# Down weights of the expert layers loaded by GpSimd's queue in place of SyncE's

## The chip, the cores and the metric

The kernel runs on one core of a Trainium2 chip. The metric is the device time of one execution in microseconds (us). A core has five engines that run their own instruction streams and meet at semaphores: TensorE (PE, with PEld for its weight loads), VectorE (DVE), ScalarE (ACT), GpSimd (POOL) and SyncE (SP). SyncE, ScalarE and GpSimd can each issue DMA transfers; every issuer has a queue of its own, and 16 DMA engines move the data of all of them.

## The reference, cut to what matters

One inference step of a two-layer decoder trunk on 512 prompt tokens and 8 sample tokens, 1024 wide, all in float32. Layer 0 mixes tokens by latent attention, layer 1 by causal pooling; each layer then applies a mixture of 16 experts, of which a router picks two per token:

```python
def moe(x, w_router, router_bias, w_gate, w_up, w_down):
    B, S, D = x.shape
    t = x.reshape(B * S, D)
    combine = route(t, w_router, router_bias).astype(x.dtype)
    h = jax.nn.silu(jnp.einsum('td,edf->tef', t, w_gate)) * jnp.einsum('td,edf->tef', t, w_up)
    y = jnp.einsum('tef,efd->td', h * combine[:, :, None], w_down)
    return y.reshape(B, S, D)
```

Per expert and layer, w_gate and w_up are 1024 x 512 and w_down is 512 x 1024, 2 MB each. After each part, x becomes LayerNorm(ALPHA * x + f(x)).

## The kernel before, in words

The kernel writes each engine's stream by hand, one function per engine (`sp`, `pe`, `pool_e`, `act`, `dve`), with semaphores between them. No scheduler changes the order: an engine executes what its function issues, in that order.

The expert part of a layer works in tiles. A tile is 96 token rows (CAP) of one expert. Sixteen tiles are the sixteen experts; further tiles take the rows of experts with more than 96, which these inputs don't need in this trace (16 tiles a layer, 8 turns of a loop over `u` with `s` = 0, 1 in it, tile number 2u + s).

- Routing (VectorE, `route`) makes the row numbers, the table `tile_ids` and the count `n_half`. GpSimd then scatters the token rows to `expert_rows` in HBM by ten indirect transfers (line 1087).
- ScalarE's queue loads the rows of a tile in four pieces (line 1256), VectorE transposes them (1724).
- TensorE does for each tile the gate product (line 919, with eight transposes of the tile before at 905 in its midst), the up product (929) and the down product (940). VectorE and ScalarE form silu(gate) * up, copy results out of PSUM, and ScalarE's queue stores the tile's rows to `expert_out` (1281).
- After a layer's last tile GpSimd gathers two rows per token from `expert_out` (1107 in layer 0, 1116 in layer 1) and the norm follows.

The weights lie in two buffers, `ring[0]` and `ring[1]`, each with room for one gate, one up and one down matrix (`wg`, `wu`, `wd`). Tile (u, s) reads buffer 1 - s. Each third is loaded again as soon as its product is done: `gate_ps`, `up_ps` and `down_ps` count TensorE's finished products, and `wg_ld`, `wu_ld`, `wd_ld` count what has landed, 16 per transfer. TensorE waits for `wd_ld` ahead of the down product. So a transfer is issued two tiles ahead of its use.

All three are issued by SyncE in `load_expert` (line 464): wait until the gate third is free, issue gate (468), wait, issue up (472), wait, issue down (476). The first two experts of a layer are loaded ahead of the loop (483, 484 in layer 0, 493 and 499 in layer 1). The gate and up loads read 16 KB runs of HBM per partition (`"a (p k) f -> p (a k) f"`), the down load four rows of 4 KB (`"a (k p) d -> p (a k) d"`). In layer 1, SyncE waits for the gathers to land (492) before the first expert, and for layer 0's norms (495) before the second.

GpSimd's stream before the change, from the end of attention on: load `wpool` (1077), then per layer wait for the row numbers and for the norm, scatter (1087), wait, in layer 0 load gains and offsets (1094, 1095), read `n_half` (1098), wait until the last tiles are stored (1100), gather (1107 or 1116), in layer 0 wait for the norms and load further gains (1133, 1134). `hold` is a wait that GpSimd also counts.

Of the kernel before, what the change touches and what calls it, by code (L numbers as in the profile page):

```python
# [12 lines left out]
P = 128  # L13
NT = SEQ // P + 1
# [8 lines left out]
BATCHES = DB // 2  # L23
# [108 lines left out]
def build(nc, t, consts_shape, place):  # L132

    ctx = ExitStack()
    with ctx:
# [260 lines left out]
        def _(sp):  # L396
# [64 lines left out]
            sp.wait_ge(pv_ps, 2)  # L461
            load_pages(sp, 3, 0, page_ld[0])

            def load_expert(L, e, s, gate_free=None, up_free=None, down_free=None):
                q = S[L]
                if gate_free:
                    sp.wait_ge(*gate_free)
                sp.dma_start(wg[s], t["w_gate"][L, bass.ds(e, 1), :, :].rearrange("a (p k) f -> p (a k) f", p=P)
                             ).then_inc(q["wg_ld"][s], 16)
                if up_free:  # L470
                    sp.wait_ge(*up_free)
                sp.dma_start(wu[s], t["w_up"][L, bass.ds(e, 1), :, :].rearrange("a (p k) f -> p (a k) f", p=P)
                             ).then_inc(q["wu_ld"][s], 16)
                if down_free:
                    sp.wait_ge(*down_free)
                sp.dma_start(wd[s], t["w_down"][L, bass.ds(e, 1), :, :].rearrange("a (k p) d -> p (a k) d", p=P)
                             ).then_inc(q["wd_ld"][s], 16)


            for L in range(2):  # L480
                q = S[L]
                if L == 0:
                    load_expert(0, 0, 1, gate_free=(pv_ps, BATCHES + 1))
                    load_expert(0, 1, 0, gate_free=(mix_ps, NT), down_free=(lg_ps, 1))
                else:
                    sp.wait_ge(S[0]["xeT_set"], 2 * nh + 1)
                    sp.wait_ge(S[0]["xe_ld"][1], 64 * (nh + 1))
                    sp.dma_start(pscale, bcast(t["pool_scale"][0])).then_inc(st_ld, 16)
                    sp.dma_start(state[0:DB * CTX, :], t["state_pool"][0].rearrange("b c d -> (b c) d")).then_inc(st_ld, 16)

                    for slot, rows in ((0, 64), (1, 64), (2, 32)):
                        sp.wait_ge(gath[slot], rows)
                    load_expert(1, 0, 1, (S[0]["gate_ps"][0], nh), (S[0]["up_ps"][0], 2 * nh), (S[0]["down_ps"][0], 2 * nh))

                    sp.wait_ge(ln_out[0], 2 * NT)
                    sp.dma_start(t["o_pool_p"][0, 0, :, :], X[P - CTX:P, 3, :]).then_inc(pool_out, 16)
                    sp.dma_start(t["o_pool_s"][0, :, CTX - 1, :], X[0:DB, 4, :]).then_inc(pool_out, 16)

                    load_expert(1, 1, 0, (S[0]["gate_ps"][1], nh), (S[0]["up_ps"][1], 2 * nh), (S[0]["down_ps"][1], 2 * nh))
                sp.wait_ge(tab_set, 2 * L + 2)  # L500
                nh = sp.value_load(n_half[0:1, 0:1], min_val=E // 2, max_val=TILES // 2)
                with sp.Fori(1, nh) as u:
                    for s in range(2):
                        ex = sp.value_load(tile_ids[0:1, bass.ds(2 * u + s, 1)], min_val=0, max_val=E - 1)
                        load_expert(L, ex, 1 - s, (q["gate_ps"][s], u), (q["up_ps"][s], 2 * u), (q["down_ps"][s], 2 * u))
            sp.wait_ge(ln_out[1], NT + 1)
            sp.dma_start(t["o_y_s"][:, 0, :], X[0:DB, 4, :]).then_inc(out_st, 16)
            for i in range(4):
# [521 lines left out]
        def _(pool_e):  # L1030
# [45 lines left out]
            hold(pool_e, uv_ps, 1)  # L1076
            pool_e.dma_start(wpool, t["w_pool"][0].rearrange("g (k p) d -> p (g k) d", p=P)).then_inc(wp_ld, 16)

            for L in range(2):
                q = S[L]  # L1080

                hold(pool_e, idx_set, 2 * (L + 1))
                hold(pool_e, zero_st, 16 * (PAIRS - 1))
                hold(pool_e, ln_out[L], NT)
                for i in range(NT):
                    for idx in (idx_a, idx_b):
                        pool_e.indirect_dma_start(  # L1087
                            xs[:, :], bass.IndirectOffsetOnAxis(ap=idx[0:rows_of(i), i:i + 1], axis=0),
                            X[0:rows_of(i), i, :], None).then_inc(scat, 16)
                hold(pool_e, scat, 160 * (L + 1))  # L1090
                if L == 0:

                    hold(pool_e, q["xeT_set"], 1)
                    pool_e.dma_start(gb[:, 0, :], bcast(t["ln1_g"][1])).then_inc(gb_ld[1][0], 16)
                    pool_e.dma_start(gb[:, 1, :], bcast(t["ln1_b"][1])).then_inc(gb_ld[1][0], 16)

                hold(pool_e, tab_set, 2 * L + 2)
                nh = pool_e.value_load(n_half[0:1, 0:1], min_val=E // 2, max_val=TILES // 2)
                for s in range(2):
                    hold(pool_e, q["y_st"][s], 16 * nh + 16)  # L1100

                def gather(i):
                    n, s = rows_of(i), i % 3
                    if i >= 3:
                        hold(pool_e, ln_z[L], NT + i - 2)
                    for idx, y in ((idx_a, ya), (idx_b, yb)):
                        pool_e.indirect_dma_start(y[s][0:n, :], None, yd[:, :],
                                                  bass.IndirectOffsetOnAxis(ap=idx[0:n, i:i + 1], axis=0)).then_inc(gath[s], 16)

                if L == 1:  # L1110
                    hold(pool_e, q["xe_ld"][0], 64 * (nh + 1))
                    hold(pool_e, q["xe_ld"][1], 64 * (nh + 1))
                    for i in (4, 0, 1, 2, 3):
                        n = rows_of(i)
                        for idx, y in zip((idx_a, idx_b), yl[i]):
                            pool_e.indirect_dma_start(y[0:n, :], None, yd[:, :],  # L1116
                                                      bass.IndirectOffsetOnAxis(ap=idx[0:n, i:i + 1], axis=0)
                                                      ).then_inc(last_gath[i], 16)
                    continue
                for i in range(3):  # L1120
                    gather(i)

                hold(pool_e, q["xe_ld"][1], 64 * (nh + 1))
                gather(3)
                if L == 0:
                    gather(4)
                for i in range(NT if L else 0):
                    shift(L, i)
                    if i == 0:
                        gather(4)  # L1130
                if L == 0:
                    hold(pool_e, ln_out[0], 2 * NT)
                    pool_e.dma_start(gb[:, 2, :], bcast(t["ln2_g"][1])).then_inc(gb_ld[1][1], 16)
                    pool_e.dma_start(gb[:, 3, :], bcast(t["ln2_b"][1])).then_inc(gb_ld[1][1], 16)
# [709 lines left out]
```

## Time and profile before

| | us |
|---|---|
| median of 3 runs | 1184.1 |
| lowest and highest | 1182.64 and 1200.41 |
| profiled execution | 1180.57 |
| its span in the trace | 1178.8 |
| layer 0's expert products (first to last) | 417.4 to 696.1 |
| layer 1's last down product ends | 1137.6 |

All times in rows are microseconds from the span's start, of the one profiled execution. The profile's page gives busy times and shares, the DMA queues (q1 is SyncE's, q10 ScalarE's, q0 GpSimd's, called software_dynamic), the chain of work that ended last, and groups of instructions. A DMA transfer is shown by its issue on the queue of its engine, by the time from the issue to its landing, and by its packets on the 16 DMA engines. The DMA share of a stretch is the mean busy share of those 16 and can read a little over 1. "issue" in place of a releaser means that nothing in the profile explains the wait.

### The profile page before, as it was taken

Reading aid. Unit: us, or ns where it says so; the run is one execution under the profiler, and the core shown is the slowest. Engines: PE = TensorE matmul, PEld = TensorE weight load, DVE = VectorE, ACT = ScalarE, POOL = GpSimd, SP = SyncE. Lnnn points to the kernel's source line nnn. Section 1 sums busy time; section 2 is a strip of 40 time slices with the busy share of each in tenths; the row PEclk is TensorE's granted clock in tenths of the full one; section 3 lists DMA queues with packets and bytes.
Section 4 is the critical chain, followed back from the end, with each engine's and each line's share of the span. In section 5 each row is a group of like instructions: output and inputs, shape, how many; then the busy total and the mean of one; then the engine's idle time right before and its main releaser. Section 6 shows DMA issues by size and latency. Waiting matters only on the chain.

```text
span 1178.8 us, 35974 instructions
## 1 busy us (share of the span) xinstructions
PE 983.8 (83%) x15825; PEld 848.9 (72%) x15825; DVE 380.8 (32%) x825; ACT 193.3 (16%) x439; POOL 95.3 (8%) x179
## 2 busy tenths in 40 slices
PE   7989999899896089999999964934995996978985
PEld 6667777644663078999999964833995996978972
DVE  1334444423453411211212128961121121211117
ACT  1234434400231020100010011112000000000010
POOL 0011211330010300000000012002000000000012
PEclk9999999999897589999999995856997998998997
DMA  9413425534025979999999967705996997997815
GB/s 334 167 54 106 145 84 152 159 102 119 10 73 229 380 244 370 380 403 386 383 386 385 397 206 286 303 22 181 378 391 246 362 410 262 359 396 249 312 46 211
DMA packets 80274, 296.67 MB, mean 252 GB/s; under 512 B 10200, under 2 KB 40288, under 8 KB 71871
## 3 DMA queue, kind: packets, MB, share of 16 engines
q1 hardware_dynamic: 52343, 246.53, 56.1%
q10 hardware_dynamic: 19712, 26.75, 7.2%
q0 software_dynamic: 8144, 22.29, 5.6%
q8 instruction: 60, 0.98, 0.3%
q14 instruction: 15, 0.12, 0.0%
HBM read 255.88 MB, written 40.11 MB: 251 GB/s over the span
## 4 chain that ended last, share of the span: by engine, by line
PE 77%; DVE 9%; issue 6%; DMA 4%; POOL 2%; ACT 1%; SPq 1%; ACTq 0%; POOLq 0%; DVEq 0%
PE PS L919 16%; PE PS L940 14%; PE PS L929 14%; PE PS L837 5%; PE PS L596 4%; PE PS L905 3%; PE PS L643 3%; PE PS L659 3%; PE PS L552 2%; PE PS L652 2%; PE PS L574 2%; POOL expert_rows L1087 2%; PE PS L750 1%; PE PS L616 1%; PE PS L633 1%
## 5 line engine op out<-in xcount | busy, mean ns | idle before, releaser
L919 PE MATMUL PS<-arena,ring 128*64 128x96 f32 x4096 | 190.4, 253 | 89.3 <-DVE arena L1724 52.9
L919 PEld LDWEIGHTS PS<-arena,ring 128*64 128x64 f32 x4096 | 179.3, 141 | 97.4 <-issue 97.4
L929 PE MATMUL PS<-arena,ring 128*64 128x96 f32 x4096 | 175.9, 246 | 4.5 <-issue 4.5
L940 PE MATMUL PS<-arena,ring 128*64 128x96 f32 x4096 | 176.1, 246 | 2.3 <-issue 2.2
L929 PEld LDWEIGHTS PS<-arena,ring 128*64 128x64 f32 x4096 | 171.4, 137 | 5.4 <-issue 5.4
L940 PEld LDWEIGHTS PS<-arena,ring 128*64 128x64 f32 x4096 | 171.6, 137 | 3.3 <-issue 3.2
L1724 DVE STREAM_TRANSPOSE arena<-arena 128x768 uint32<-128x768 uint32 x34 | 54.3, 1596 | 169.7 <-ACT arena L1292 140.1
L1749 DVE COPY arena<-PS 128x384 f32<-128x384 f32 x32 | 17.8, 557 | 164.5 <-PE PS L940 164.5
L1294 ACT ACTIVATE arena<-PS 128x384 f32<-128x384 f32 x32 | 15.7, 490 | 266.5 <-PE PS L940 266.5
L837 PE MATMUL PS<-ring,arena 128*128 128x512 f32 x128 | 55.7, 594 | 0.7 <-issue 0.7
L1734 DVE COPY arena<-PS 96x512 f32<-96x512 f32 x32 | 22.0, 687 | 100.6 <-PE PS L905 100.6
L1279 ACT ACTIVATE arena<-PS 96x512 f32<-96x512 f32 x32 | 18.9, 592 | 167.6 <-PE PS L905 167.6
L837 PEld LDWEIGHTS PS<-ring,arena 128*128 128x128 f32 x128 | 24.1, 190 | 30.2 <-issue 30.1
L596 PE MATMUL PS<-arena,ring 128*128 128x260 f32 x192 | 44.9, 384 | 1.0 <-POOL ring L1037 0.7
L905 PE MATMUL PS<-C,arena 128*96 128x128 f32 x272 | 40.3, 296 | 1.3 <-DVE arena L1749 1.3
L643 PE MATMUL PS<-ring 128*128 128x512 f32 (+3 forms) x128 | 38.7, 445 | 1.9 <-ACT ring L1177 1.2
L596 PEld LDWEIGHTS PS<-arena,ring 128*128 128x128 f32 x192 | 35.2, 190 | 6.0 <-POOL ring L1037 0.9
L1048 POOL DMA_DIRECT2D ring<-cache_krope x64 | 34.5, 539 | 58.5 <-issue 58.5
L1116 POOL DMA_INDIRECT arena<-expert_out,ids x10 | 10.1, 1009 | 341.6 <-issue 341.6
L1185 ACT ACTIVATE ring<-PS,small 128x512 f32<-128x512 f32 (+1 forms) x64 | 33.0, 526 | 26.5 <-DVE small L1448 26.5
L1448 DVE CUSTOM_DVE_ANT_0 PS<-PS,C 128x512 f32<-128x512 f32 (+1 forms) x64 | 30.4, 507 | 15.3 <-PE PS L643 14.8
L905 PEld LDWEIGHTS PS<-C,arena 128*96 128x96 f32 x272 | 30.8, 135 | 6.2 <-DVE arena L1749 1.7
(264 smaller groups left out, 1038.2 us busy)
## 6 DMA issues: line engine op xcount, KB each, us to landing
ring<-w_gate SPq DMA_DIRECT2D x32, 2048.0 KB, 11.5
ring<-w_up SPq DMA_DIRECT2D x32, 2048.0 KB, 12.8
ring<-w_down SPq DMA_DIRECT2D x32, 2048.0 KB, 14.5
arena<-expert_rows ACTq DMA_DIRECT2D x144, 96.0 KB, 7.8
expert_out<-arena ACTq DMA_DIRECT2D x32, 384.0 KB, 9.7
expert_rows<-ring SPq DMA_DIRECT2D x6, 1920.0 KB, 10.1
ring<-cache_ckv SPq DMA_DIRECT2D x56, 128.0 KB, 2.0
ring<-w_o SPq DMA_DIRECT2D x1, 4096.0 KB, 19.1
```

The source lines that it names most:

```text
L596: last = nc.tensor.matmul(bank(b, HALF), wuq[:, m, P * parity:P * (parity + 1)], cq[:, m, HALF * hf:HALF * (hf + 1)], start=(m == 0), stop ...
L643: nc.tensor.matmul(score(i), qT[par][:, P * i:P * (i + 1)], kT[par][:, 0:P * (i + 1)], start=True, stop=True).then_inc(s_ps, 1)
L659: last = nc.tensor.matmul(bank(3, 4, VH, off=256 * par)[at:at + 64, i, :], probT[:, i % 2, P * k + at:P * k + at + 64], V[odd][:, k, VH * ...
L837: last = nc.tensor.matmul(bank(b0 + hf)[0:n, :], oT[:, k, P * i:P * i + n], wo[:, k, 512 * hf:512 * (hf + 1)], start=(k == 0), stop=(k == ...
L905: last = nc.tensor.transpose(bank(4 + m // 4, 4, P)[0:CAP, m % 4, :], yT[:, m, :], ident)
L919: last = nc.tensor.matmul(bank(s, KF, CAP)[at:at + 64, f, :], wg[w][:, k, P * f + at:P * f + at + 64], xeT[s][:, k, :], start=(k == 0), st ...
L929: last = nc.tensor.matmul(out[at:at + 64, :], wu[w][:, k, P * f + at:P * f + at + 64], xeT[s][:, k, :], start=(k == 0), stop=(k == KD - 1))
L940: last = nc.tensor.matmul(bank(4 + m // 4, 4, CAP)[at:at + 64, m % 4, :], wd[w][:, f, P * m + at:P * m + at + 64], h[s][:, f, :], start=(f ...
L1048: pool_e.dma_start(krp[:, bass.ds(half, 1), ROPE * n:ROPE * (n + 1)], t["cache_krope"][0, bass.ds(page, 1), :, :].rearrange("a p d -> p a ...
L1185: nc.scalar.activation(prob[:, i, 0:P * (i + 1)], score(i), ACT.Exp, scale=-1.0, bias=mneg[:, c:c + 1], accum_out=rsum[:, c:c + 1]).then_i ...
L1448: v.tensor_tensor_reduce(sc, sc, causal[:, SEQ - w:SEQ], 1.0, BIG, ALU.add, ALU.min, mneg[:, 4 * par + i:4 * par + i + 1]).then_inc(min_se ...
L1724: v.transpose(xeT[s].rearrange("p m (a j) -> p a m j", j=32).bitcast(mybir.dt.uint32), xe[s].rearrange("p a (i m) -> p a m i", i=32).bitca ...
```

## The change

SyncE's `load_expert` no longer loads down weights. GpSimd gets a function `load_down`, the two first loads of layer 0 behind `wpool`, a loop like SyncE's ahead of its wait for the last stores, and the two first loads of layer 1 behind the last gather of layer 0. Semaphores, buffers and shapes of the transfers stay as they are. `gate` and `up` loads stay on SyncE. Behind the change, line numbers from 475 on differ from those before (by up to 12).

```diff
-            def load_expert(L, e, s, gate_free=None, up_free=None, down_free=None):
+            def load_expert(L, e, s, gate_free=None, up_free=None):
...
-                if down_free:
-                    sp.wait_ge(*down_free)
-                sp.dma_start(wd[s], t["w_down"][L, bass.ds(e, 1), :, :].rearrange("a (k p) d -> p (a k) d", p=P)
-                             ).then_inc(q["wd_ld"][s], 16)
...
-                    load_expert(0, 1, 0, gate_free=(mix_ps, NT), down_free=(lg_ps, 1))
+                    load_expert(0, 1, 0, gate_free=(mix_ps, NT))
...
-                        load_expert(L, ex, 1 - s, (q["gate_ps"][s], u), (q["up_ps"][s], 2 * u), (q["down_ps"][s], 2 * u))
+                        load_expert(L, ex, 1 - s, (q["gate_ps"][s], u), (q["up_ps"][s], 2 * u))
...
+            def load_down(L, e, s):
+                pool_e.dma_start(wd[s], t["w_down"][L, bass.ds(e, 1), :, :].rearrange("a (k p) d -> p (a k) d", p=P)
+                                 ).then_inc(S[L]["wd_ld"][s], 16)
+
...
+                if L == 0:
+                    hold(pool_e, pv_ps, BATCHES + 1)
+                    load_down(0, 0, 1)
+                    hold(pool_e, lg_ps, 1)
+                    load_down(0, 1, 0)
...
+                with pool_e.Fori(1, nh) as u:
+                    for s in range(2):
+                        ex = pool_e.value_load(tile_ids[0:1, bass.ds(2 * u + s, 1)], min_val=0, max_val=E - 1)
+                        hold(pool_e, q["down_ps"][s], 2 * u)
+                        load_down(L, ex, 1 - s)
...
+                    load_down(1, 0, 1)
+                    load_down(1, 1, 0)
```

SyncE in one turn of the expert loop before (TENSOR_LOAD reads the tile's expert, `ring` is the weight buffer):

```order
L504 TENSOR_LOAD ids
L504 ISA x2
L468 ISA
L468 DMA ring<-w_gate 128x4096
L472 DMA ring<-w_up 128x4096
L476 DMA ring<-w_down 128x4x1024
```

The same half turn after the change:

```order
L500 TENSOR_LOAD ids
L500 ISA x2
L468 ISA
L468 DMA ring<-w_gate 128x4096
L472 DMA ring<-w_up 128x4096
```

The down load is gone from SyncE's queue, and nothing else moved there. GpSimd from the load of `wpool` to layer 0's gathers before:

```order
L1077 DMA arena<-w_pool 128x8x256
L1087 DMA expert_rows<-X,ids 2880x1024 x10
L1094 DMA gb<-ln_g 128x1024
L1095 DMA gb<-ln_b 128x1024
L1098 TENSOR_LOAD ids
L1098 ISA x2
L390 ISA
L1107 DMA arena<-expert_out,ids 128x1024 x6
```

GpSimd over the same stretch after:

```order
L1073 DMA arena<-w_pool 128x8x256
L1076 DMA ring<-w_down 128x4x1024 x2
L1092 DMA expert_rows<-X,ids 2880x1024 x10
...
L1106 TENSOR_LOAD ids
L1106 ISA x2
L1076 ISA
L1076 DMA ring<-w_down 128x4x1024
L1106 ISA
L1106 TENSOR_LOAD ids
L1106 ISA x2
L1076 ISA
L1076 DMA ring<-w_down 128x4x1024
L1104 REGISTER_ALU
L1104 COMPARE_AND_BRANCH
L390 ISA
```

Two down loads now stand between `wpool` and the scatters, and a loop with two down loads stands ahead of the gathers. Each loop body reads the expert first and waits for `down_ps` after it.

## Rows read from the trace of the kernel before

**Rows 1.** The page: busy us (share of span), instructions; queue: packets, MB, share.
```profile
PE 983.8 (83%) x15825; PEld 848.9 (72%) x15825; DVE 380.8 (32%) x825; ACT 193.3 (16%) x439; POOL 95.3 (8%) x179
...
q1 hardware_dynamic: 52343, 246.53, 56.1%
```

**Rows 2.** Sums by stretch: us, busy per engine, PEclk, DMA share, GB/s.
```profile
561.00:578.00 17.00, 17.00 (x398) 16.70 (x394) 3.55 (x5) 1.57 (x3) 0.00 (x0) 1.00 1.02 387
...
720.00:780.00 60.00, 48.56 (x494) 42.27 (x492) 50.98 (x68) 12.47 (x29) 2.61 (x4) 0.76 0.59 231
```

**Rows 3.** The page, DMA issues: count, KB each, median us to landing (w_gate, w_up likewise 2048).
```profile
ring<-w_down SPq DMA_DIRECT2D x32, 2048.0 KB, 14.5
arena<-expert_rows ACTq DMA_DIRECT2D x144, 96.0 KB, 7.8
expert_out<-arena ACTq DMA_DIRECT2D x32, 384.0 KB, 9.7
```

**Rows 4.** Landing of w_down: issued at 437.6, at 661.9, all of layer 1's loop.
```profile
DMA to landing us min/median/max: 11.9/11.9/11.9
...
DMA to landing us min/median/max: 28.6/28.6/28.6
...
DMA to landing us min/median/max: 11.8/13.2/14.6
```

**Rows 5.** Timeline of layer 0's loop, a down issue: start us, us, engine, line.
```profile
491.92 0.40 SPq L476 DMA_DIRECT2D ring<-w_down  x1
```

**Rows 6.** Chain that ended last, layer 0's loop: start us, us, what.
```profile
508.88 1.32 PE PS L919 x32
510.20 1.01 PE PS L905 x8
511.21 4.11 PE PS L919 x96
...
520.60 5.28 PE PS L940 x128
```

**Rows 7.** The same chain in layer 1's loop, at the first and third pause.
```profile
885.84 12.06 issue
...
1053.64 12.03 issue
1065.67 2.83 PE PS L919 x32
1068.50 1.87 PE PS L905 x8
1070.37 4.39 PE PS L919 x96
```

**Rows 8.** Waits of SyncE's queue: line, waited for, us in total, times, longest.
```profile
SPq L476 <- PE PS L940: 139.2, 28, 6.0
```

**Rows 9.** Waits of GpSimd, and its load of w_pool in the timeline.
```profile
POOL arena L1107 <- DMA expert_out<-arena: 283.9, 1, 283.9
...
369.41 0.90 POOL L1077 DMA_DIRECT2D arena<-w_pool  x1 [24.59 <-PE PS L814]
```

**Rows 10.** DMA queues in 373:376, 377:380, 381:383, 399:402, 560:594: packets, MB, share.
```profile
q1 hardware_dynamic: 60, 0.98, 77.3%
q0 software_dynamic: 49, 0.20, 18.0%
...
q0 software_dynamic: 134, 0.55, 50.5%
q1 hardware_dynamic: 131, 0.53, 45.6%
...
q1 hardware_dynamic: 188, 0.77, 97.6%
...
q0 software_dynamic: 264, 0.99, 80.8%
...
q10 hardware_dynamic: 1118, 1.57, 13.2%
```

More of the change, by code:

```diff
@@ L492, in _ @@
                         sp.wait_ge(gath[slot], rows)
-                    load_expert(1, 0, 1, (S[0]["gate_ps"][0], nh), (S[0]["up_ps"][0], 2 * nh), (S[0]["down_ps"][0], 2 * nh))
+                    load_expert(1, 0, 1, (S[0]["gate_ps"][0], nh), (S[0]["up_ps"][0], 2 * nh))
                     sp.wait_ge(ln_out[0], 2 * NT)
@@ L497, in _ @@
                     sp.dma_start(t["o_pool_s"][0, :, CTX - 1, :], X[0:DB, 4, :]).then_inc(pool_out, 16)
-                    load_expert(1, 1, 0, (S[0]["gate_ps"][1], nh), (S[0]["up_ps"][1], 2 * nh), (S[0]["down_ps"][1], 2 * nh))
+                    load_expert(1, 1, 0, (S[0]["gate_ps"][1], nh), (S[0]["up_ps"][1], 2 * nh))
                 sp.wait_ge(tab_set, 2 * L + 2)
```

## The prediction

> **What bounds the kernel now.** I read the page first for the shares [rows 1]. TensorE is busy 83% of the span, GpSimd 8%. SyncE's queue q1 carries 246.53 MB. So two things can be the limit in the expert loops, TensorE and the DMA engines, and the next view must say which.
>
> The sums by stretch of one tile (17.00 us) say both [rows 2]. In layer 0's loop TensorE is busy 17.00 of 17.00 us and the DMA engines read 1.02, at 387 GB/s. Per tile the program asks for three weight transfers of 2048 KB, four of 96 KB and one of 384 KB [rows 3]: 6.29 + 0.79 = 7.08 MB. In 17.00 us at 387 GB/s only 6.58 MB move. The DMA side is 0.50 MB, or 1.3 us, short in every tile, and TensorE doesn't wait, because it lives on what was loaded ahead. The time to landing shows that stock being used up [rows 4]: the down transfer issued at 437.6 lands after 11.9 us, the one at 661.9 after 28.6 us. They are 13 tiles apart: (28.6 - 11.9) / 13 = 1.3 us a tile, the same number by another way.
>
> How much may it take? A down transfer goes out at 491.92, just after a tile's down product, and the down product that reads it starts two tiles later, at 520.60 [rows 5, 6]: 28.7 us. The last one took 28.6. Layer 0 ends with nothing to spare, and any rearrangement that makes one kind of transfer late will be seen.
>
> Layer 1 differs. Every four tiles or so TensorE stands still for 12 us at a tile's first product (the first time at 885.84, the third at 1053.64) with "issue" as the reason [rows 7], and the DMA side catches up: its down transfers land after 11.8 to 14.6 us, half the 28.7 [rows 4].
>
> **The change, part by part.** *Removed:* 32 DMA issues and their waits on SyncE. None is on a path: an issue takes 0.40 us and then SyncE waits for TensorE, 139.2 us in all for the down buffers alone [rows 5, 8]. Its waits come in the order in which TensorE finishes (gate, up, down), so the down wait holds up no gate load. Gain: 0.
>
> *Added on GpSimd:* 32 issues and two loops. In the loops GpSimd only waited before (283.9 us up to layer 0's first gather) [rows 9], and it reads the tile's expert before it waits, so its reading is hidden. The nearest row for its cost is the 1024 KB load of line 1077, 0.90 us [rows 9] against SyncE's 0.40 us. A down load is twice as large: between 0.9 and 1.8 us, so 0.5 to 1.4 us later than now. Until the 28.7 us are used up that is hidden; afterwards it counts once, because transfers are then limited by bandwidth. I take 0.5 us. The loops end when the last tile but two is through its down product, long before the gathers of line 1107 may start, which wait for the last store.
>
> *Moved at the start of layer 0:* GpSimd issues line 1077's load at 369.41 [rows 9], so expert 0's down load goes out near 370.5, a few us later than now; it is needed only after the first gate and up products, some 50 us on. Expert 1's goes out after the router as before. The ten scatters of line 1087 now stand behind it in one queue, but before the change they shared the engines with the same bytes, and the total is the same: 0, at worst 1 us. *In layer 1:* both first down loads are issued after the last gather, before and not after the norms, when the engines are 59% busy [rows 2]: 0.
>
> *What the queues do to each other* carries the sum. Before, gate, up and down stand in one queue in the order of need. After, two queues share the engines. At 373 to 376 us this happened already, with GpSimd's load beside gate and up loads [rows 10]: q1 60 packets and 0.98 MB, q0 49 packets and 0.20 MB. At 377 to 380 q1 also carried small packets: 131 to 134 packets, 0.53 to 0.55 MB. So the engines take a packet of each in turn, whatever its size; gate and up go in packets of 16.3 KB and down in packets of 4.1 KB, so down gets a fifth of what the weights get.
>
> Per tile and engine there are 16 gate and up packets and 32 down packets. A large one takes 0.773 x 3 x 16 / 60 = 0.62 us, a small one of q0 0.180 x 3 x 16 / 49 = 0.18 us. Sixteen turns of both take 12.7 us, and rows in and out take 13.2% of a tile [rows 10], 2.2 us. There remain 2.1 us, or 12 more small ones: 28 of 32. Gate and up are always served and the whole shortfall falls on down. Down then moves 2.10 - 0.50 = 1.60 MB a tile, and its time to landing grows by 0.50 / 1.60 x 17 = 5.3 us a tile; in the early tiles, where landing times grew by nearer 1.0 us, by about 4. From 13 us for tile 2 it passes 28.7 us after four or five tiles, at tile 6 or 7. From there to tile 14 (behind it no gate or up load is left to compete) TensorE waits for down weights, at the pace of the DMA side. Eight tiles x 1.3 us = 10.4 us. TensorE can't win that back: each wait comes when gate and up of the next tile have landed, and the engines run dry sooner at the end.
>
> Does a down packet itself cost more on q0? At 373 to 376 it took 0.176 us; on q1 alone at 381 to 383, 0.976 x 2 x 16 / 188 = 0.166 us [rows 10]. Ten ns x 32 packets is 0.3 us a tile, 2.4 us in eight. Bounds: nothing below; above, 0.181 at 377 to 380 against 0.147 at 399 to 402 [rows 10], 1.1 us a tile and 13 us over the twelve tiles then affected. I take 2.4, the row in which q0 stands beside large packets, as it will.
>
> The waits come in lumps rather than 1.3 us at a time, and a long one lowers the clock. After the 12.03 us pause the first products take 2.83, 1.87 and 4.39 us, in place of 1.32, 1.01 and 4.11 from 508.88 on [rows 6, 7]: 2.7 us. I count it once, bounds 0 and four times.
>
> Sum for layer 0: 10.4 + 2.4 + 0.5 + 2.7 = 16.0 us. Layer 1: its down transfers grow from 11.8 to 14.6 over the three tiles between pauses, 0.9 us or 0.35 MB a tile. On down alone that is 0.35 / 1.75 x 17 = 3.4 us a tile: from 13 to about 23 us, and the next pause empties the queues. Under 28.7: 0, with some room. Profiled execution: 1180.6 + 16.0 = 1196.6 us. The median of the runs before lies 3.5 us above the profiled one, so I forecast 1200 us, +1.4%. A difference under 2% can hardly be told from none here.
>
> The Trainium skill, "DMA: Bandwidth & Descriptors", section "Queues, rings and completion order", says that an engine goes round the queues at packet granularity; by this rule the trace agrees with its 60 and 49 packets. The same skill's "SBUF — State Buffer", section "SBUF: two separate sides", warns that VectorE's two-port copies keep GpSimd from writing descriptors; beside the moment of issue stands only line 1749's short copy out of PSUM, so by that rule the sum would grow by no more than that copy's length; no run here shows it.
>
> **Rivals.**
> *A, not slower:* the shortfall is shared evenly. If the engines are simply kept full and down's last packets are served no later than now, the end of layer 0 is set by the bytes, which are the same. For it: the DMA share is 1.02 throughout and the total is unchanged. Against: the 0.98 to 0.20 MB. It decides if down's time to landing stays under 28.7 us to the end. Price 0: 1184. The skill's section "Issuing engines are not separate DMA queues" says just this, that another issuer saves only issue time.
> *B, much slower:* a down packet on q0 costs the upper bound, 13 - 2.4 = 11 us more in layer 0; with four clock drops 8 us more; and layer 1 passes 28.7 us before each pause, 3 x 5 = 15 us. For it: 0.181 against 0.147, and layer 1's margin of 6 us. Against: the load of line 1077 reads rows of 256 elements, 1 KB, where down rows have 4 KB. With the first whole and the others by half: 1200 + 22 = 1222; with all of them 1234.
> *C, faster:* layer 1's 12 us pauses change. For: three pauses of 12 us, 36 us in all [rows 7]. Their rows name no releaser; if they are fetches of TensorE's instructions through busy DMA queues, a second busy queue may lengthen or shorten them. Against: TensorE's program is the same, and so is the traffic. If all go: 1184 - 36 + 16 = 1164; if only shorter, within 2%.
> *D, the edit has no effect:* excluded by the order; the down loads do stand on GpSimd's queue.
>
> **How the numbers follow.** Forecast 0.60, A 0.20, B 0.16, C 0.04. The range goes from A's 1184 to 1224, just past B's 1222. Slower by over 2% means over 1208: all of B and a quarter of the forecast, 0.31. Faster by over 2% is at most part of C: 0.03. The rest, 0.66, is within 2%.
>
> **What would show it.** In the changed profile q1 drops to about 179 MB and q0 rises to about 89. Gate loads of layer 0 land in about 8 to 10 us even late, where the last down load took 28.6; down loads pass 28 us from tile 6 to 8 on; the first product of line 940 shows waits on w_down of 1 to 7 us, about 12 in all, and none before tile 5. Layer 0's last down product ends about 16 us later; layer 1's keeps its length with three 12 us pauses. It is wrong if gate and down landing times grow alike (A), or if layer 1 shows waits on w_down (B).

## The result and the profile after

The changed kernel takes 1189.4 us (median of 20 runs, 1183.65 to 1205.95) against 1185.2 us (median of 20, 1180.04 to 1200.41): 1.004 times as long, 95% interval 1.0024 to 1.0055. The ratio leaves out the few executions that took over 1.5% longer than the fastest of their kernel. A second series of the same kernel on another chip gave 1.0089 (1.0073 to 1.0106, 6 runs). The forecast was 1200 us, +1.4%: the direction is right, the size three and a half times what the first series gave and half as much again as the second. Both lie in the forecast's range and within 2%.

The profiled execution of the changed kernel took 1188.56 us, with a span of 1186.8 us. I read it in the order of the prediction. The page first, for the queues and the landing times. It answers to [rows 1, 3].

```profile
PE 984.7 (83%) x15825; PEld 847.1 (71%) x15825; DVE 380.1 (32%) x825; ACT 193.7 (16%) x439; POOL 118.7 (10%) x211
...
q1 hardware_dynamic: 35447, 179.42, 39.8%
q0 software_dynamic: 25040, 89.40, 21.0%
...
ring<-w_gate SPq DMA_DIRECT2D x32, 2048.0 KB, 11.2
ring<-w_up SPq DMA_DIRECT2D x32, 2048.0 KB, 13.6
ring<-w_down POOLq DMA_DIRECT2D x32, 2048.0 KB, 23.0
arena<-expert_rows ACTq DMA_DIRECT2D x144, 96.0 KB, 6.9
expert_out<-arena ACTq DMA_DIRECT2D x32, 384.0 KB, 12.7
```

The bytes have moved as forecast, to 179 and 89 MB, and the median down load now lands after 23.0 us in place of 14.5. TensorE's busy time hasn't changed, so what was added is waiting.

Where does it wait? The list of waits of layer 0 (420 to 704 us) gives engine, line, what was waited for, total, times, longest. Lines 915, 925 and 936 are now the gate, up and down products, 1736 VectorE's transpose of the next tile's rows, 1756 its first multiplication for the down product.

```profile
DVE arena L1736 <- DMA arena<-expert_rows: 35.0, 5, 7.7
...
PE PS L925 <- issue: 3.2, 1, 3.2
PE PS L936 <- DVE arena L1756: 3.1, 3, 1.1
PEld PS L936 <- DVE arena L1756: 3.9, 4, 1.3
```

No row says that TensorE waits for `w_down`. It waits about 1 us, three times, for VectorE (the weight loads' row, PEld, has 3.9 us in four waits), and VectorE waited for the rows that ScalarE's queue brings. This view puts a wait for several semaphores down to one of them, so the landing times have to be read beside it. The chain and the timeline show it in one tile (start us, us, what):

```profile
613.72 28.42 DMA arena<-expert_rows
642.17 0.06 DVE arena L1736
642.23 1.44 issue
643.66 0.42 DVE arena L1756
644.09 0.04 issue
644.13 3.54 PE PS L936 x80
```

```profile
642.17 1.57 DVE L1736 STREAM_TRANSPOSE arena<-arena 128x768 uint32<-128x768 uint32 x1 [7.70 <-DMA arena<-expert_rows]
...
644.13 5.50 PE L936 MATMUL PS<-arena,ring 128*64 128x96 f32 x128 [1.09 <-DVE arena L1756]
```

A load of 96 KB is 28.42 us on its way. VectorE's transpose stands ahead of its multiplication, so it holds that up, and the down product starts 1.09 us late. The rows aren't all of it: the down weights of the same tile, issued at 614.8, land 28.6 us later, at 643.4, and would have held the product up for about half of that time anyway.

The landing times of the two late kinds, for transfers issued in 612 to 629 us (down weights, then rows), and the down weights of all of layer 1's loop. Before, layer 1's row was the last of [rows 4].

```profile
DMA to landing us min/median/max: 28.6/28.6/28.6
...
DMA to landing us min/median/max: 20.8/26.7/28.4
...
DMA to landing us min/median/max: 11.4/22.4/25.0
```

The sums by stretch of one tile, which answer to [rows 2]: us, busy per engine, clock, DMA share, GB/s.

```profile
527.00:544.00 17.00, 17.00 (x398) 16.70 (x396) 3.55 (x5) 1.58 (x3) 0.74 (x1) 1.00 1.00 387
...
561.00:578.00 17.00, 17.00 (x398) 16.70 (x396) 3.55 (x5) 1.58 (x3) 0.74 (x1) 1.00 1.02 400
578.00:595.00 17.00, 17.00 (x398) 16.70 (x396) 3.54 (x5) 1.58 (x3) 0.74 (x1) 1.00 1.03 407
...
629.00:646.00 17.00, 15.91 (x367) 15.42 (x362) 3.32 (x5) 1.58 (x3) 0.74 (x1) 1.00 1.02 398
```

In the same stretch, 561 to 578 us, the engines move 400 GB/s where they moved 387. Behind the pause of the first turn, TensorE's busy time falls short of the 17.00 only in the last tiles. Its clock stays at 1.00.

Layer 1's loop keeps its three pauses (the chain; before, 12.06 and 12.03 us in [rows 7]):

```profile
891.58 12.39 issue
...
976.40 12.34 issue
...
1059.83 12.32 issue
```

Taken apart at the first gate product and the last down product of each layer, the two profiled executions differ so:

| stretch, us | before | after |
|---|---|---|
| start to layer 0's first gate product | 417.4 | 419.7 |
| layer 0's loop | 278.4 | 283.2 |
| between the loops | 117.4 | 116.2 |
| layer 1's loop | 324.1 | 324.5 |

I call the second row "layer 0's loop" below. The distance from one tile's first gate product to the next's (in the timeline) says where its 4.8 us stand. Counted from 0, tiles 2 to 10 take 17.00 us each, before and after. Tiles 11 to 14 take 17.29, 18.31, 18.21 and 18.26 us after and 17.00 before: 4.1 us in four tiles. The rest, about 1 us, stands in the first two tiles, at an "issue" pause; these two take 41.2 us together after and 40.3 before, but 39.7 in the kernel below that has the change in layer 0 only, so this part can't be put to the change. Of the stretch before the loop the change alters only where two down loads are issued; whether its 2.3 us are chance was tested.

### The profile page after: what moved, and what is told of

It is laid out like the page before. It is cut to its first block, busy times and chain, and to the rows that moved or that the text cites. A ratio compares the mean times of both kernels' runs of the same rounds, so it can differ in the third digit from the quotient of the medians.

```text
span 1186.8 us, 36172 instructions
## 1 busy us (share of the span) xinstructions
PE 984.7 (83%) x15825; PEld 847.1 (71%) x15825; DVE 380.1 (32%) x825; ACT 193.7 (16%) x439; POOL 118.7 (10%) x211
## 4 chain that ended last, share of the span: by engine, by line
PE 70%; DVE 10%; DMA 9%; issue 7%; POOL 2%; ACT 1%; SPq 1%; ACTq 0%; POOLq 0%; DVEq 0%
PE PS L915 14%; PE PS L936 13%; PE PS L925 13%; DMA arena<-expert_rows 5%; PE PS L833 5%; PE PS L592 4%; PE PS L639 3%; PE PS L901 3%; PE PS L655 3%; PE PS L548 2%; PE PS L648 2%; PE PS L570 2%; POOL expert_rows L1092 1%; DVE small L1587 1%; PE PS L612 1%
## 5 line engine op out<-in xcount | busy, mean ns | idle before, releaser
L1076 POOL DMA_DIRECT2D ring<-w_down x32 | 24.0, 751 | 539.1 <-PE PS L936 472.8
L592 PE MATMUL PS<-arena,ring 128*128 128x260 f32 x192 | 47.6, 400 | 1.1 <-POOL ring L1033 0.8
L639 PEld LDWEIGHTS PS<-ring 128*128 128x128 f32 x128 | 23.6, 195 | 17.0 <-issue 11.2
```

The costliest lines, as they stand in the source:

```text
L592: last = nc.tensor.matmul(bank(b, HALF), wuq[:, m, P * parity:P * (parity + 1)], cq[:, m, HALF * hf:HALF * (hf + 1)], start=(m == 0), stop ...
L639: nc.tensor.matmul(score(i), qT[par][:, P * i:P * (i + 1)], kT[par][:, 0:P * (i + 1)], start=True, stop=True).then_inc(s_ps, 1)
```

## Experiments

Each ratio is to the kernel before, run on the same chip in the same series.

**The changed kernel and the kernel before once more.** No edit.

> The changed kernel once more, unchanged, for a second profile of it beside the variants of this group. If its pauses in layer 0 come from the change, they come again: the last tiles' down landings stand near 28 us, TensorE waits about 1 us three or four times ahead of the down product, and layer 0's loop is 283 us, 4 to 5 longer than the kernel before. If they are chance of one execution, this profile shows a loop of 278 to 280 us. The time should be 1.003 to 1.005 of the kernel before either way.

> The kernel before, unchanged, for a second profile of it: how much the stretches scatter without any change. If layer 0's loop is 278 us again (within 1), the 4.7 to 5.8 us found in the changed kernel's loops belong to the change. The stretch before layer 0's first product was 417.4 us in the first profile and 418 to 426 in the variants, which alter nothing in it: if that is scatter, it comes out above 418 here. The ratio is 1.000.

Measured: after again, 1.0089 (1.0073 to 1.0106), layer 0's loop 284.2 us; before again, 1.0009 (0.9995 to 1.0024), loop 277.9 us, start 420.6 us. So the loop's loss comes again (4.8 and 5.8 us; in tiles 2 to 14 alone 4.1 and 4.8), and the 2.3 us at the start are scatter. One more thing came out: this execution of the changed kernel, 1202.36 us long, has a fourth 12 us pause in layer 1 (third row). It is one of the six of its series; the mean of the other five is 1.0073 of the kernel before's.

```profile
891.46 12.37 issue
976.00 12.29 issue
1027.41 11.52 issue
1110.46 12.69 issue
```

**One layer at a time.** The down loads by GpSimd in one layer, by SyncE in the other. SyncE's part of the first kernel (the second has `L == 0` there):

```diff
-                if down_free:
+                if L == 1:
+                    if down_free:
```

> Down weights by GpSimd's queue in layer 0 only, by SyncE's in layer 1. Theory 1 (the whole loss is the late rows and down weights at the end of layer 0's loop): the ratio stays at 1.004, like the full change, layer 0's loop near 283 us, layer 1's 324. Theory 2 (the loss lies outside layer 0's loop, in what GpSimd's queue does at the change between the layers and in layer 1): the ratio falls to 1.000 to 1.001 though layer 0's loop still shows its pauses.

> Down weights by SyncE's queue in layer 0, by GpSimd's in layer 1 only: the other half of the pair. Theory 1 (all of the loss is in layer 0's loop): ratio 1.000, layer 0's loop 278 us as before, layer 1's loop 324 us with its three pauses of 12 us. Theory 2 (loss outside layer 0's loop): ratio 1.003 to 1.004.

Measured: layer 0 only 1.0063 (1.0045 to 1.008), loop 283.0 us, tiles 10 to 14 late by 5.3 us together; layer 1 only 1.0027 (1.0003 to 1.005), loop 277.4 us, no tile from 2 to 14 over 17.00 us. Their excesses add up to the 1.0089 of the same series. Most of the loss is layer 0's; a small part isn't, or lies at the limit of the measurement.

**All three weights on GpSimd's queue.** SyncE's loop is gone; GpSimd asks for gate, up and down in the order of need.

> All three weight loads of every expert on GpSimd's queue, in the order gate, up, down: one queue again, but the software one. If the split into two queues is what costs (R and D alike), rows land in 17 us or less as before the change, gate, up and down landing times rise together to 26 to 29 us, ratio 1.000 to 1.002. If loads by GpSimd cost in themselves (0.75 us per issue in place of 0.40, descriptors written by a program), the ratio is 1.004 or more and landing times pass 28.7 us.

Measured: 1.0045 (1.0018 to 1.0073). The ratio alone would say that nothing was won. But layer 0's loop takes 275.3 us, TensorE's only gap over 0.5 us in it is one of 0.54 us ahead of a down product at its end, and the landing times are those of before (table below). GpSimd as the issuer, at three issues a tile, doesn't make layer 0's tiles late. Two queues do. The loop is shorter than before's because the "issue" pauses of its first two tiles are missing (36.2 us for the two in place of 40.3). The lost time stands in this execution at the start (425.7 us, longer than in any other profile) and in layer 1 (327.6 us). So this isn't a repair: the kernel as a whole is as slow as the changed one.

**Up in place of down on GpSimd's queue.**

```diff
-                sp.dma_start(wu[s], t["w_up"][L, ...]).then_inc(q["wu_ld"][s], 16)
+                pool_e.dma_start(wu[s], t["w_up"][L, ...]).then_inc(S[L]["wu_ld"][s], 16)
```

> The up weights are asked for by GpSimd's queue, gate and down by SyncE's. As many bytes stand in the two queues as in the changed kernel, but in GpSimd's they now come in 16 KB runs and in SyncE's half in 4 KB ones. Theory of packet turns (the queue with the short packets gets too small a share): the transfers of SyncE's queue are now the late ones, down lands 20 us or more after its issue in layer 0's last tiles while up stays under 15, and the loop is 3 to 8 us longer than before. Rival (whatever stands in GpSimd's queue gets behind): up lands 20 us or more after its issue, down under 16. Second rival (a transfer alone in its queue is late because it is asked for while the other two are still moving): up lands at about 20 us in both layers, but no wait follows from it and the ratio is 1.000 to 1.002.

Measured: 1.0043 (1.0025 to 1.006), loop 278.1 us. Up, in large packets and alone in its queue, lands after 12 us; SyncE's queue carries the lateness, gate 28.1 and down 28.9 us. That is the theory of packet turns as to who is late. Of its 3 to 8 us the low end came, and the loop's length hides it: tiles 12 to 14 take 3.3 us more than 17.00 each, with 2.3 us of waits for gate weights, while the first two tiles take 36.8 us in place of 40.3. Both rivals fell: what stands in GpSimd's queue isn't late as such.

**All weight packets of one size.** Gate and up are asked for in four parts each, so that a packet carries 4 KB, on before and on after.

```diff
-                sp.dma_start(wg[s], ...(p k) f -> p (a k) f...).then_inc(q["wg_ld"][s], 16)
+                for j in range(4):
+                    sp.dma_start(wg[s][:, 2 * j:2 * j + 2, :], ...[:, 2 * j:2 * j + 2, :]).then_inc(q["wg_ld"][s], 16)
```

> The kernel before, with the gate and up weights of an expert each asked for in four parts of 0.5 MB, so that their packets carry 4 KB, as those of the down weights do. Control for the next. Either theory: same time as before, ratio 1.000 to 1.003, layer 0's loop 278 to 280 us, down landing near 15 us after its issue. If short packets cost rate in themselves, the loop is longer: at 0.98 MB in 60 packets against 240, a rise in the overhead shows here alone.

> The changed kernel with the same edit: down weights in GpSimd's queue, gate and up in SyncE's, all packets of 4 KB now. Theory of packet turns (a queue's share goes by the size of its packets): down no longer gets behind, lands within 18 us of its issue in the last tiles of layer 0 instead of 28, its waits are gone, and layer 0's loop is within 1 us of the control's. Rival (down is late because GpSimd's queue, or a queue of its own, serves it slowly): down still lands at 25 to 28 us, the loop is 4 to 6 us longer than the control's.

Measured: control 1.0058 (1.0032 to 1.0084), loop 280.1 us; with down on GpSimd's queue 1.009 (1.0064 to 1.0117), loop 285.2 us. Half of the theory held: down lands after 16.9 us to the end and the rows after 7.6. The other half failed: the loop is still 5.1 us longer than its control's, and tiles 9 to 14 take 8.2 us more than 17.00 each (the control's 1.1, and 1.6 more at its last down product, which waits for down weights that land at 696.4). The waits of that kernel in 420 to 704 us say why (917 and 927 are its gate and up products):

```profile
PE PS L927 <- DMA ring<-w_up: 4.0, 5, 1.4
PE PS L917 <- DMA ring<-w_gate: 1.9, 3, 0.9
```

With equal packets it is up and gate that come too late. The size of the packets decides who is late, and neither way removes the loss. What the equal packets did restore is the rows. In two tiles (560 to 594 us) ScalarE's queue moved this in the changed kernel, then with equal packets; before it was the 1118 packets of [rows 10]:

```profile
q0 software_dynamic: 952, 3.77, 29.4%
q10 hardware_dynamic: 951, 1.42, 11.5%
```

```profile
q10 hardware_dynamic: 1120, 1.57, 13.4%
```

The queue with the shortest packets fell behind as well while SyncE's queue held large packets only: 951 packets here and 952 in the second execution of the changed kernel, against 1118 and 1068 in the two of the kernel before. The landing times of the rows, 26 us in place of 12, say it more plainly.

**Half of up left out.** The first 1.05 MB of each up load isn't asked for in the loops (the products use what stands there from an earlier expert), on before and on after. The queues stay as they are, and up's packets carry 8 KB in place of 16 in both kernels; the demand falls to 6.03 MB in 17.00 us, or 355 GB/s, under what the engines move elsewhere.

```diff
-                sp.dma_start(wu[s], ...)
+                k0 = 0 if up_free is None else 4
+                sp.dma_start(wu[s][:, k0:, :], ...[:, k0:, :])
```

> The kernel before without the first half of each up load in the loops (1.05 MB of 7.08 MB a tile is not asked for; the products use what an earlier expert left there). A tile then asks for 6.03 MB in 17.6 us, 343 GB/s, under the 385 to 391 GB/s that the engines moved in the late windows. Control for the next. Expected: landings stay flat along layer 0's loop, down within 13 us; no wait falls away that before had, so layer 0's loop is 277 to 278 us and the ratio 0.998 to 1.001. If the layer 1 pauses or the first turn's pauses hang on weight traffic, the time falls further.

> The changed kernel with the same half of each up load left out. Theory of the deficit (the change costs only because the loop asks for more than the engines move, and with two queues the shortfall no longer falls on the transfer that is needed last): layer 0's loop equals the control's within 1 us, down lands within 16 us throughout, and the ratio to the control is 1.000 to 1.001. Rival (a load through GpSimd's queue costs in itself, by its slower issue or by what GpSimd does to others): the ratio to the control stays 1.003 to 1.004 without one late landing.

Measured: 0.9892 (0.9869 to 0.9915) for the control and 0.9907 (0.9876 to 0.9938) with down on GpSimd's queue, medians 1172.16 and 1172.32 us. The loops are 276.6 and 274.4 us. The sums by stretch of the second:

```profile
561.00:578.00 17.00, 17.00 (x396) 16.70 (x392) 3.55 (x5) 1.57 (x3) 0.76 (x2) 1.00 0.94 356
...
595.00:612.00 17.00, 17.00 (x396) 16.70 (x392) 3.55 (x5) 1.57 (x3) 0.76 (x2) 1.00 0.97 352
```

With a DMA share of 0.94 to 0.97 each tile from 2 to 14 takes 17.00 us in both kernels, and TensorE waits for no weights. This pair settles the cause in layer 0: same issuer, same two queues, no shortfall, no late tile. The times agree with it but couldn't show it by themselves: with six runs each, the difference of the two kernels is 0.9 us with an interval of about 4.6 to either side, and the loss looked for is 4 to 5 us. The 2.2 us between the loops are the pause of the first two tiles again. I had expected the control at 0.998 to 1.001, and it is faster: layer 1's loop fell from 324 to 314 us, its pauses from 12 to about 10. So the length of those pauses goes with the weight traffic.

**Where layer 0 has slack for another reason.** The down weights loaded in 16 KB packets, on before and on after; this needs every fourth column in the gate and up products, and so slows TensorE.

```diff
-                wg[w][:, k, P * f + at:P * f + at + 64]
+                wg[w][:, k, KF * at + f:KF * (at + 64):KF]
```

> The kernel before with the same 16 KB runs for down, all on SyncE's queue: the control for the one above. Both theories: down moves in 8 x 0.615 = 4.9 us per engine in place of 32 x 0.162 = 5.2 us, so landing times at the end of layer 0 stay under 28 us and the time is the same, ratio 0.998 to 1.002. If picking columns with a step of four slows TensorE's weight loads, the mean of a weight load rises above 137 ns and both down16 kernels are slower by the same amount, which would have to be taken off.

> The changed kernel with the down weights read in runs of 16 KB, four adjacent rows to a partition (gate and up columns are picked with a step of four to match), so that GpSimd's queue has 8 large packets per engine and tile in place of 32 small ones. Theory R: each of the 24 row packets per engine now waits for two large packets, 24 x 1.3 = 31 us, over the 27 us that rows have; rows land after 30 us and more, and the ratio to before rises to 1.010 or more. Theory D: down weights get an equal share, land in under 15 us, and no wait is left, ratio 1.000 or below.

Measured: 1.1558 (1.1512 to 1.1604, 1370.86 us) and 1.1583 (1.1538 to 1.1629, 1373.09 us). As a test of the packets it failed: a weight load of the gate product takes 217 ns in place of 141, layer 0's loop grows from 278 to 351 us, and the DMA engines have time to spare (share 0.85 and 0.93 from 561 to 578 us). It serves as a second run without a shortfall: layer 0's loop is 350.8 us without the change and 350.7 with it. Layer 1 has seven pauses of 11 to 12 us in both, at every second tile, and in these two executions its loop is 4.3 us longer with the change, of which 3 us stand in the pauses; the kernels' medians differ by 2.2 us. Why isn't shown.

**VectorE's transpose behind its multiplications**, in the changed kernel, so that late rows no longer hold up the tile in hand.

```diff
                     dve.wait_ge(q["sg_set"], tl + 1)
-                    dve.wait_ge(q["xe_ld"][1 - s], 64 * (u + 1 + s))
-                    turn_rows(1 - s)
...
                     v.tensor_tensor(h[s][:, KF - 1, :], ...)
+                    dve.wait_ge(q["xe_ld"][1 - s], 64 * (u + 1 + s))
+                    turn_rows(1 - s)
```

> The changed kernel, with VectorE's transpose of the next tile's rows moved behind the two products silu(gate) * up, so that late rows no longer hold up the down product. Theory R (the rows that ScalarE's queue loads come late, because their small packets take turns with two weight queues): TensorE's waits on the product (1.1 us, three or four times at the end of layer 0) vanish, layer 0's loop falls from 283.4 to 279 to 281 us, ratio to before 1.000 to 1.002. Theory D (the down weights are what comes late, as predicted, and the product is only the name seen): the waits ahead of the down product stay, now with no product behind them, loop 283 us or more, ratio 1.004 as before the edit.

Measured: 1.0038 (1.001 to 1.0067), loop 280.7 us, down landing at 29.0 and rows at 27.0 us. One profile shows 2.5 us won, of which 1.2 in tiles 2 to 14; the times don't confirm it. Inconclusive as a repair. It does show that the rows are only one of two late kinds, for the predicted wait on down weights can be seen here. Line 1757 is VectorE's last multiplication (the landing is of the load issued at 594.6):

```profile
622.63 0.25 DVE L1757 TENSOR_TENSOR arena<-arena,PS 128x96 f32<-128x96 f32 x1 [0.80 <-PE PS L925]
...
623.75 1.46 PE L936 MATMUL PS<-arena,ring 128*64 128x96 f32 x30 [1.17 <-DVE arena L1757]
...
DMA to landing us min/median/max: 29.0/29.0/29.0
```

The view names VectorE, but VectorE was done at 622.88. The down weights landed at 623.7, and the product started at 623.75. The other wait, 1.28 us up to 659.25, ends in the same way, with the load issued at 630.0 that takes 29.1 us.

**GpSimd's loop without its loads**, on the kernel before.

> The kernel before, with GpSimd running the changed kernel's loop of expert reads and waits in both layers and asking for nothing. Theory: 1.000 to 1.001, both loops as before. Rival for the part of the loss that stands outside layer 0's loop (GpSimd's own instructions, their fetches and their reads of the table disturb): 1.002 to 1.004, with a longer layer 1.

Measured: 1.0018 (0.999 to 1.0046), loop 277.6 us. Nothing that can be told from none. Its profiled execution (1201.84 us) again has four pauses, though its weights all come by SyncE's queue; the fourth doesn't need the change.

**Layer 1's loop moved in TensorE's program**, on the kernel before.

```diff
+                if L == 1:
+                    for _ in range(512):
+                        pe.wait_ge(router_ld, 32)
                 pe.wait_ge(tab_set, 2 * L + 2)
```

> The kernel before with 512 fulfilled waits ahead of TensorE's code of layer 1's expert loop, which moves that code by some 256 instructions and does nothing else. It asks what the three 12 us pauses of layer 1's loop hang on. If on where the loop lies in the instruction stream, their number changes: none would give 1150 us, six 1220. If on anything else, the three pauses stay, and the time is that of before or up to 8 us more for the waits themselves.

Measured: 1.0022 (1.0004 to 1.0039), three pauses of 12 us at the same tiles. This shift doesn't move them.

Landing times of transfers issued from 595 to 631 us (median us), two tiles near the end of layer 0, beside its loop and what tiles 2 to 14 take beyond 17.00 us each. With 4 KB packets, gate and up are the median of their four parts.

| kernel | gate | up | down | rows | loop | beyond 17.00 |
|---|---|---|---|---|---|---|
| before | 22.7 | 23.5 | 25.3 | 12.3 | 278.4 | 0 |
| all on GpSimd's queue | 24.6 | 24.4 | 25.6 | 9.7 | 275.3 | 0.4 |
| after | 11.6 | 13.5 | 28.6 | 26.3 | 283.2 | 4.1 |
| after again | 11.4 | 13.4 | 28.2 | 26.6 | 284.2 | 4.8 |
| up on GpSimd's queue | 28.1 | 12.2 | 28.9 | 13.2 | 278.1 | 3.3 |
| 4 KB packets, before | 18.5 | 17.7 | 23.8 | 7.0 | 280.1 | 1.1 |
| 4 KB packets, after | 19.2 | 21.6 | 16.9 | 7.6 | 285.2 | 8.2 |
| half of up left out, before | 8.0 | 5.9 | 9.8 | 2.8 | 276.6 | 0 |
| half of up left out, after | 10.3 | 9.1 | 16.3 | 4.5 | 274.4 | 0 |

The table is the mechanism. Where all weights stand in one queue, whoever issues them, the three kinds are equally late, 23 to 26 us, and hardly any is past what it may take. Where they are split and the demand is whole, one kind is early and gains nothing by it, while another comes to its limit, and the last column grows. The loop's length alone misleads, since it also holds the pause of the first two tiles.

## Why the prediction was wrong in size

**What bounds the kernel: right.** The shortfall in layer 0 and a stock that is used up to the last were the whole matter there; without the shortfall no tile of layer 0 is late (the half loads).

**Removed and added instructions: right, 0 and small.** GpSimd's issue takes 0.74 us, under the 0.9 to 1.8 us I bounded it by. All loads on that queue leave layer 0's tiles at 17.00 us up to the last two. *The start: not seen*, 417.4 and 420.6 us in two executions of the kernel before, 419.7 and 418.7 of the changed one.

**"The engines take a packet of each in turn": right in direction.** Gate and up land early, down late, up alone in GpSimd's queue early, and with packets of one size down is no longer the late one. But gate lands after 11.6 us, not 8 to 10.

**"Rows in and out take 13.2% of a tile": the step that failed first.** I took ScalarE's queue as always served and set its share aside before I shared out the rest. Yet it has the shortest packets of all, 96 KB in rows of 1 KB, and by my own rule gets one turn for each 16.3 KB packet of SyncE's queue. Before, that queue also held down's 4.1 KB packets, so turns came quickly. Afterwards it held large ones only: 951 packets in two tiles in place of 1118, and rows landed after 26 us in place of 12. So "the whole shortfall falls on down" was wrong. Part of it fell on the rows. Down landed after 26.7 us in the load issued at 580.8, for tile 10, and after 28.6 us in the one issued at 614.8, for tile 12 (the trace lacks the one for tile 11); I had put that at tile 6 or 7. And the waits came mostly through VectorE.

**"Eight tiles x 1.3 us = 10.4 us": mis-sized, the largest miss.** The 1.3 us for a tile that waits was right (1.2 to 1.3 us in three of the four); the eight was wrong: the tiles that waited were four in the first profile and five in the second, as the stock lasted longer. The shortfall, which I had worked out at 387 GB/s, wasn't constant: with large and small packets side by side the engines moved about 399 GB/s late in the loop. 7.08 MB in 17.00 us are 416 GB/s; at 399 the shortfall is 0.30 MB or 0.75 us a tile, three fifths of the 0.50 MB. My own packet count had said as much: it left 4 of 32 small packets unserved, 4 x 0.18 = 0.7 us a tile, and I went on with 0.50 MB all the same. Where the rate did stay at 386 GB/s, with 4 KB packets, six tiles were late by 8.2 us. Measured for this term: 4.1 and 4.8 us, in place of 10.4.

**"Does a down packet itself cost more on q0?", 2.4 us: nearly nothing.** From 560 to 594 us a packet of q0 took 0.294 x 34 x 16 / 952 = 0.168 us, beside the 0.166 on q1 alone and the 0.176 that I took, and the engines as a whole moved more, not less. **The clock, 2.7 us: not paid.** The waits are near 1 us, and the granted clock stays at 1.00. **GpSimd's later issue, 0.5 us, counted once:** too small to see.

So layer 0's 16.0 us were 4.8 to 5.8, of which 4.1 to 4.8 are late tiles.

**Layer 1, 0: right in its profile.** Down lands after 22.4 us at the median and 25.0 at most, where I had said 23, under its 28.7, and the pauses are unchanged. With the changed queue in layer 1 only, the time was still 1.0027 (1.0003 to 1.005).

**The rivals.** A (shared evenly, not slower) fell: the interval excludes 1, and gate and down don't grow alike. But its argument that the bytes are the same is why so little was lost. The Trainium skill, "DMA: Bandwidth & Descriptors", section "Issuing engines are not separate DMA queues", says that another issuing engine saves only issue time; the runs agree in layer 0 as far as there is slack (no late tile with half of up left out), and with the engines full it costs. B (much slower) and C (the pauses change) didn't come.

**What stays open.** Two kernels without late tiles in layer 0 still measured 1.0027 (layer 1 only) and 1.0045 (all on GpSimd's queue), and the control with 4 KB packets, with no weights on GpSimd's queue, 1.0058. GpSimd's loop alone gave 1.0018 with 1 in its interval. Where these 3 to 5 us stand I could not separate from the 2 to 3 us by which the stretches of single executions scatter, and no run says whether GpSimd's queue has a part in them. With all on GpSimd's queue they are as much as the whole change costs, so layer 0's late tiles, 4.1 to 4.8 us, match the loss of the whole in size, but that they are all of it isn't shown. Nor is it shown why the rate rises to 399, or why the same change measured 0.4% on one chip and 0.9% (0.7% without the execution with four pauses) on another.

## What to carry to other kernels

Where DMA demand stands above what the engines move, one queue in the order of need spread the shortfall over all transfers; a second queue broke that order though it added no byte, and the kinds that were then early gained nothing. To say who will be late, count the packets of every queue, the small helper's too, since the turns went by packets here: the rows, with the shortest packets, fell behind once the longest stood beside them. And a busy share of 1.01 to 1.03 doesn't fix the GB/s: here it went with 380 to 407, so a shortfall of 7% must not be carried through a sum as a constant. Last, when a view names one engine for a wait on several semaphores, set its end beside the landing times before you believe it.

## What the runs showed that I hadn't expected

- The same loads at the same DMA share (1.00 to 1.03) move 387 GB/s with all weights in one queue, 386 with 4 KB packets in either arrangement, and 395 to 407 late in the loop with 16 KB packets in one queue and 4 KB packets in the other.
- A transfer of 96 KB can take 28.42 us to land, as long as one of 2048 KB, though all that stood ahead of it on ScalarE's queue was the other three parts of its tile, a store and three loads of the tile before.
- Picking every fourth column of a 4-byte weight tile raises a TensorE weight load of 128x64 from 141 to 217 ns (groups by line).
- Layer 1's pauses are shorter with less weight traffic (10.39, 10.21 and 9.53 us with half of up left out in place of 12.06, 12.19 and 12.03). A fourth appeared in two executions, of 1202.36 and 1201.84 us, one of them with all weights on SyncE's queue. With the slower products of the 16 KB down packets there are seven. What decides on them isn't shown.
